# A conditioning product moved from TensorE to VectorE in a three-block transformer kernel

## The reference, cut to what matters

```python
def ada_params(cond, w_ada, b_ada):
    m = jax.nn.silu(cond) @ w_ada + b_ada
    return jnp.split(m[..., None, :], 6, axis=-1)      # shift, scale, gate, twice
...
def modulate(x, g, shift, scale):
    return rmsnorm_2(x, g) * (1 + scale) + shift
...
    x = x + g_m * y
    x = x + g_f * ec_moe(modulate(x, norm_ffn[l], sh_f, sc_f), ...)
```

## Time and profile before

| | |
|---|---|
| three runs | 2081.14, 2081.37, 2082.59 us (median 2081.37) |
| the profiled execution | 2083.17 us, its span on the core 2081.4 us |
| TensorE busy | 1675.8 us (81%) |
| weight loads of TensorE | 788.9 us (38%) |
| VectorE busy | 424.6 us (20%) |
| ScalarE busy | 310.4 us (15%) |
| GpSimd busy | 74.4 us (4%) |
| dense stages | 0 to 249, 720 to 993, 1458 to 1606 us |
| moved from main memory | 709.09 MB |

### The profile page before, as it was taken

How to read it: one execution, slowest core, us unless ns; L and a number is a source line. 1 busy time by engine, 2 the same in 40 slices (tenths; PEclk the granted TensorE clock), 3 DMA queues, 4 the chain that set the end, 5 groups by cost and what they waited for, 6 DMA issues and landing times.

```text
span 2081.4 us, 22500 instructions
## 1 busy us (share of the span) xinstructions
PE 1675.8 (81%) x9286; PEld 788.9 (38%) x9286; DVE 424.6 (20%) x941; ACT 310.4 (15%) x723; POOL 74.4 (4%) x113
## 2 busy tenths in 40 slices
PE   7999988888888689999786776776997776767766
PEld 3456544433343244664331321321784231313212
DVE  2234311111111142154210111111213111111101
ACT  2123111111111121251110100100101110100000
POOL 1300000000000042000000000000000000000000
PEclk9978999999999989999988988988998998988988
DMA  9464699999999942464999999999742999999997
GB/s 348 162 242 162 242 413 422 421 421 422 423 422 421 405 173 74 157 247 176 384 420 420 420 425 420 420 422 414 279 162 81 380 424 421 421 420 425 420 420 324
DMA packets 129436, 711.46 MB, mean 342 GB/s; under 512 B 5568, under 2 KB 5824, under 8 KB 104640
## 3 DMA queue, kind: packets, MB, share of 16 engines
q1 hardware_dynamic: 128496, 707.02, 83.9%
q10 hardware_dynamic: 848, 3.15, 0.4%
HBM read 709.09 MB, written 1.05 MB: 341 GB/s over the span
## 4 chain that ended last, share of the span: by engine, by line
DMA 46%; PE 45%; DVE 2%; ACT 2%; issue 2%; POOL 1%; ACTq 0%; POOLq 0%; SPq 0%; DVEq 0%
DMA ring<-in_moe_w_down 33%; DMA ring<-in_w_down 8%; PE bank L446 8%; PE bank L1252 6%; DMA ring<-in_moe_w_up 5%; PE bank L1207 5%; PE bank L1894 4%; PE bank L566 4%; PE bank L1123 4%; PE bank L1276 4%; PE bank L362 2%; PE bank L382 1%; PE bank L694 1%; PE bank L308 1%; PE bank L1648 1%
## 5 line engine op out<-in xcount | busy, mean ns | idle before, releaser
L1207 PE MATMUL bank<-ring,arena 128*32 128x512 f32 x3072 | 401.1, 650 | 150.8 <-DMA ring<-in_moe_w_up 108.3
L1252 PE MATMUL bank<-ring,arena 128*32 128x512 f32 x1536 | 225.7, 714 | 157.8 <-DMA ring<-in_moe_w_down 117.1
L1276 PE MATMUL bank<-arena 128*128 128x512 f32 x512 | 235.3, 602 | 30.9 <-DVE arena L1331 17.4
L1207 PEld LDWEIGHTS bank<-ring,arena 128*32 128x32 f32 x3072 | 93.4, 113 | 384.3 <-issue 242.7
L1298 DVE COPY arena<-bank 128x512 f32<-128x512 f32 x96 | 66.4, 692 | 672.1 <-PE bank L1207 672.1
L1252 PEld LDWEIGHTS bank<-ring,arena 128*32 128x32 f32 x1536 | 49.3, 120 | 291.3 <-issue 177.7
L446 PE MATMUL bank<-ring,hT 128*128 128x512 f32 (+1 forms) x352 | 153.0, 591 | 3.1 <-DVE hT L323 1.6
L1290 ACT ACTIVATE arena<-bank 128x512 f32<-128x512 f32 x96 | 57.3, 597 | 624.8 <-PE bank L1207 624.8
L1276 PEld LDWEIGHTS bank<-arena 128*128 128x128 f32 x512 | 92.3, 190 | 138.2 <-issue 94.0
L1123 PEld LDWEIGHTS bank<-arena,xn 128*128 128x128 f32 x512 | 124.1, 333 | 7.1 <-issue 3.3
L1123 PE MATMUL bank<-arena,xn 128*128 128x128 f32 x512 | 123.0, 400 | 1.0 <-DVE arena L1155 0.7
(11 more groups left out here) (226 smaller groups left out, 1207.4 us busy)
## 6 DMA issues: line engine op xcount, KB each, us to landing
ring<-in_moe_w_gate SPq DMA_DIRECT2D x64, 2048.0 KB, 24.2
ring<-in_moe_w_up SPq DMA_DIRECT2D x64, 2048.0 KB, 26.3
ring<-in_moe_w_down SPq DMA_DIRECT2D x64, 2048.0 KB, 26.9
ring<-in_w_gate SPq DMA_DIRECT2D x32, 2048.0 KB, 19.2
ring<-in_w_up SPq DMA_DIRECT2D x32, 2048.0 KB, 21.6
ring<-in_w_down SPq DMA_DIRECT2D x32, 2048.0 KB, 24.3
ring<-in_ada_w SPq DMA_DIRECT2D x24, 2048.0 KB, 10.2
ring<-in_w_in SPq DMA_DIRECT2D x6, 2048.0 KB, 20.3
```

The lines of the kernel that those rows point to most:

```text
L1207: last = nc.tensor.matmul(AA[hf if M.nf == 2 else up][32 * j:32 * j + 32, :], xgT[:, x + kk, a:a + C], w[:, kq + j, hf * NC:(hf + 1) * NC] ...
L1252: last = nc.tensor.matmul(AA[n][32 * j:32 * j + 32, :], act_s[:, b, q * C:(q + 1) * C], w[:, j, n * NC:(n + 1) * NC], start=(kk < 4), stop ...
L1276: nc.tensor.matmul(Y[2 * t + n][:, :], wselT[:, e % 2, t * P:(t + 1) * P], z_s[:, n * NC:(n + 1) * NC], start=(e == 0 and M.fresh), stop=( ...
```

## The change

The product is computed on VectorE. For each section and vector, eight instructions add weight rows times a number per partition into an accumulator of 128 x 1024 (`ada_add_dve`): the first a `tensor_scalar`, the others `scalar_tensor_tensor` with the weights and the accumulator in on-chip memory. There are 14 such jobs (sections 0 and 1 twice), 112 instructions. What stays on TensorE is the sum over the 128 partitions: two matmuls of 512 columns with ones for a gate, eight transposes for a shift or scale, which VectorE then reduces with two instructions. ScalarE's copies go. An accumulator lies in a buffer of its own or in one that is free then.

A weight item is now half of a section, all 1024 columns of 512 rows, so that a descriptor moves 4 KB where it moved 2 KB. The slot is released by VectorE's last add that reads it. The items are spread between the projection chunks of all three dense stages: sections 0 to 2 in block one, 3 to 7 in block two, 8 to 11 in block three (which had none). The adds are written into the step lists: in a query or key unit one before the unit and one inside `rooted`, between VectorE's sum and its wait for GpSimd's root; two to four in the value units; some in the attention loops. The loads of the gate biases for block three and of the context rows are issued later, since their buffers serve as accumulators.

```diff
-EARLY = 4
+JOBS = [(s, c) for s in range(12) for c in range(2 if s < 2 else 1)]
+ADDS = [(s, c, k) for s in range(12) for half in range(2) for c in range(2 if s < 2 else 1) for k in range(4 * half, 4 * half + 4)]
...
+    after = [[(0, 0)], [(0, 1)], [], [(1, 0)], [(1, 1)], [(2, 0), (2, 1)]]
+    for n, name in enumerate(CHUNKS1):
+        proj("proj1", n, ("w_in", W_IN_COLS[name]))
+        for sec, half in after[n]:
+            conditioning(sec, half)
...
+    after = [[(3, 0)], [(3, 1), (4, 0)], [(4, 1), (5, 0)], [(5, 1), (6, 0)], [(6, 1), (7, 0), (7, 1)]]
...
+    after = [[(8, 0), (8, 1)], [(9, 0)], [(9, 1), (10, 0)], [(10, 1), (11, 0), (11, 1)], [], []]
...
-        def rooted(ins, sums, n):
+        def rooted(ins, sums, n, meanwhile=None):
 
             dve_step(ins)
             sums_added(sums, n)
+            if meanwhile is not None:
+                meanwhile()
             nc.vector.wait_ge(roots_done, chain_at["sums"])
...
+        def ada_add_dve(count):
+
+            dve = nc.vector
+            for _ in range(count):
+                sec, c, k = ADDS[chain_at["adds"]]
+                chain_at["adds"] += 1
+                i = ITEM["ada", sec, k // 4]
+                j = job_at[sec, c]
+                acc, w, by = accs[acc_of[j]], ring[i % SLOTS][:, :, :].rearrange("p a b -> p (a b)")[:, (k % 4) * D:(k % 4 + 1) * D], condT[:, k, c:c + 1]
+                if k % 4 == 0:
+                    wait_item(dve, i)
+                if k:
+                    dve.wait_ge(ada_added, add_at[sec, c, k - 1])
+                    ins = dve.scalar_tensor_tensor(acc, w, by, acc, ALU.mult, ALU.add)
+                else:
...
+                    ins = dve.tensor_scalar(acc, w, by, None, ALU.mult)
+                ins.then_inc(ada_added, 1)
...
+        def ada_sum_pe(j, banks):
...
+            if sec % 6 in (G_M, G_F):
                 for n in range(2):
+                    last = nc.tensor.matmul(banks[n][:, :], const("ones"), acc[:, n * NC:(n + 1) * NC], start=True, stop=True)
             else:
                 for k in range(KD):
+                    last = nc.tensor.transpose(banks[k // 4][:, (k % 4) * P:(k % 4 + 1) * P], acc[:, k::KD], ident)
...
+            for n in range(2):
+                ins = dve.tensor_reduce(dst[:, 4 * n:4 * n + 4], banks[n][:, :].rearrange("p (k r) -> p k r", r=P), AX.X, ALU.add)
...
         def steps1():
             for u in range(len(units1)):
+                if u:
+                    yield "ada_add", 1 if u < 9 else 4
                 yield "proj", u
                 if u >= 2:
                     yield "tr", u - 2
+                if u in (8, 10):
+                    yield "ada_sum", (8, 10).index(u)
+                if u in (9, 11):
+                    yield "ada_use", (9, 11).index(u)
+            yield "ada_add", 4
...
+                if u in (3, 8, 24):
+                    yield "ada_sum", 2 + (3, 8, 24).index(u)
+                if u in (6, 11, 27):
+                    yield "ada_use", 2 + (6, 11, 27).index(u)
+                if u % 2 and u < 16:
+                    yield "ada_add", 1
...
         def steps2():
             for u in range(NU2):
+                yield "ada_add", 1 if units2[u]["kind"] == "qk" else 2
                 yield "proj", u
...
+                if u in (6, 10, 14):
+                    yield "ada_sum", 5 + (6, 10, 14).index(u)
...
+                if u in (1, 7):
+                    yield "ada_sum", 8 + (1, 7).index(u)
+                if u in (2, 8):
+                    yield "ada_use", 8 + (2, 8).index(u)
+                if u < 4:
+                    yield "ada_add", 1
...
                 last.then_inc(item_done, 1)
+                if i >= 2:
+                    ada_sum_pe(8 + i, TR)
             out_pe(2, 0, mix3, [(mix_done, 8)])
...
+            ada_add_dve(12)
             for n in range(2):
...
+                if n == 0:
+                    ada_use_dve(10, TR)
+                    ada_add_dve(6)
+                    ada_use_dve(11, TR)
+                    ada_add_dve(8)
...
+                    if what[0] == "ada":
+                        w = ada_w[what[1]][:, what[2] * D:(what[2] + 1) * D].rearrange("(p k) n -> p k n", p=P)
```

More of the change, by code:

```diff
@@ new lines, in transformer_blocks @@
+        add_at = {a: n + 1 for n, a in enumerate(ADDS)}
+        job_at = {j: n for n, j in enumerate(JOBS)}
+        accs = {"own": ada_acc[:, :], "ctx0": gate_rows[:, 1, 0, :], "ctx1": gate_rows[:, 1, 1, :], "end": arena[:, ARENA - D:ARENA],
+                "odd": arena[:, 9472:9472 + D]}
+        acc_of = ["own", "ctx0", "ctx1", "end", "own", "own", "ctx1", "own", "ctx1", "own", "odd", "own", "odd", "own"]
+        for sec in range(12):
+            for half in range(2):
+                released[ITEM["ada", sec, half]] = (ada_added, add_at[sec, 1 if sec < 2 else 0, 4 * half + 3])
@@ L395, in ada_use_dve @@
+                dve.tensor_tensor(g[:, NC:D], g[:, NC:D], banks[1][:, :], ALU.add).then_inc(ada_used, 1)
                 return
-            sums = AB[0][:, 0:2 * KD].rearrange("p (k c) -> p c k", c=2)
             m = (0 if sec < 3 else 2) + sec % 3
-            both = [(mod[:, l, m, :], 0)] + ([(mod_ctx[:, m, :], 1)] if s < 2 else [])
-            for n, (dst, c) in enumerate(both):
-                ins = nc.vector.tensor_tensor(dst, sums[:, c, :], col(f"b{l}{sec}"), ALU.add)
-                if sec % 3 == 1:
-                    dve_step(ins)
-                    gain = col(f"norm_mix{l}" if sec < 3 else f"norm_ffn{l}")
-                    ins = nc.vector.scalar_tensor_tensor(dst, dst, 1.0, gain, ALU.add, ALU.mult)
+            dst = mod_ctx[:, m, :] if c else mod[:, l, m, :]
@@ L405, in ada_use_dve @@
+            for n in range(2):
+                ins = dve.tensor_reduce(dst[:, 4 * n:4 * n + 4], banks[n][:, :].rearrange("p (k r) -> p k r", r=P), AX.X, ALU.add)
+            dve_step(ins)
+            ins = dve.tensor_tensor(dst, dst, col(f"b{l}{sec}"), ALU.add)
+            if sec % 3 == 1:
+                dve_step(ins)
+                gain = col(f"norm_mix{l}" if sec < 3 else f"norm_ffn{l}")
+                ins = dve.scalar_tensor_tensor(dst, dst, 1.0, gain, ALU.add, ALU.mult)
             ins.then_inc(ada_used, 1)
@@ L476, in post_dve @@
                 dve.wait_ge(sqs, q + 1)
[L477 removed]
+                rooted(nc.vector.tensor_reduce(s8, view(sq[:, q % 2, 0:n]), AX.X, ALU.add), s8, HD, meanwhile)
                 if q >= 2:
@@ L1046, in route2_dve @@
                 dve_step(v.match_replace(workT, best8, workT, -1.0))
-                if n == 1 and section is not None:
-                    ada_use_dve(section)
             dve_step(v.memset(onesT, 1.0))
@@ L1068, in route2_pe @@
             last.then_inc(af_tr, 1)
-            if section is not None:
-                ada_sum_pe(section)
-                ada_mm_pe(section + 1)
             pe.wait_ge(af_slot, l + 1)
```

243 lines of the change are left out of this document (102 added, 141 removed).

## The result

The changed kernel takes **2089.83 us** (median of 7 runs, 2088.32 to 2093.18), the kernel before in the same comparison 2081.25 (7 runs): ratio 1.0041, 95% interval 1.003 to 1.0053, so it is slower by 6 to 11 us. The forecast was 2080.5 (no change) in a range of 2059 to 2095. The range holds the time; that the kernel would become slower was missed. The profiled execution took 2088.69 with a span of 2086.6, 5.2 more than the span before; it lies 1.1 under its median, the one before lay 1.8 above the median of its first three runs, which is why the medians stand further apart (8.6 us) than the profiles. What follows accounts for the 5.2.

A forecast was written before the change was run, and what follows sets the result against it. Expert stages were taken as bound by weight loads, so only dense stages, mostly TensorE-bound, counted: -22.5 + 14 + 3.5 + 3.7 = -1.3 us. From the 2081.37 median that gave 2080.1, stated as 2080.5, range 2059 to 2095.

The forecast's parts named there:

- Block 1, attention loop: First attention loop: products, ScalarE copies and small sums go, so 81.5 us becomes 59, a gain of 22.5 us.
- nine microseconds at half clock: First attention loop, second half: 3.5 heads go at half clock, the other 12.5 at full, together 26.5 us.
- half clock to the end of that loop: Rival, first attention loop: without the conditioning products the clock stays at half, loop 73.5 us, kernel time 2095 us; chance 0.20.
- bound for full clock throughout: First attention loop: lower bound of 54 us if TensorE kept full clock all through, against 59 forecast.
- Block 1, projections: Block 1 before its attention loop: adds hold GpSimd and delay the last chunk's load, a loss of 14 us.
- powers of 2.9 us: Sign in the profile after: GpSimd's powers in the units take near 2.9 us instead of 1.64.
- Block 2: Whole second dense stage: projections +9.8 and +3.5, attention loop -7.5, routing -2.3, together +3.5 us.
- Block 3: Third dense stage: four sums join a TensorE that is never idle, a loss of 3.7 us.
- Routing of block 1: Block 1's routing: removed products and sums save about 3 us, half clock costs 3, so nothing; bounds -3 and +2.
- the adds do not hold GpSimd: Rival: VectorE's adds leave GpSimd free; block 1 regains 11.4 us, block 2 about 9, kernel time 2060 us; chance 0.17.
- full clock: Rival: full clock through the first attention loop, 54 us instead of 59, kernel time 2075.5 us; chance 0.18.
- fuller rings: Rival: earlier expert loads let expert stages start ahead, 5 us per stage at most, kernel time 2071 us; chance 0.05.

The follow-up runs named there:

- e4: Changed kernel with block 2's first four units free of adds, their eight adds moved to later units and sums moved back; ratio 1.0019 against the kernel before.
- e1: Changed kernel plus four bursts of four 512-column matmuls, results thrown away, before heads 7, 13, 18, 29 of the first attention loop; ratio 1.0042 against the kernel before.
- e7: Changed kernel plus three bursts of four 512-column matmuls at heads 10, 18 and 26 of the first attention loop; ratio 0.9999 against the kernel before.
- e10: Changed kernel with loads reordered, adds and sums re-placed (none beside heads 18 to 31), bursts of four matmuls at head 18, two at 26; 2071.5 us, ratio 0.9949.
- e3: Changed kernel with only block 1's load order altered, so the last projection chunk no longer waits for the 16th add; ratio 1.0012 against the kernel before.
- e11: Changed kernel with block 2's first eight adds summing in two PSUM banks, one section's product left out; 2083.19 us, one execution only.
- e6: Changed kernel with block 1's loads reordered, adds moved away from busy rope units, and three bursts of four matmuls at heads 10, 18, 26; ratio 0.9966.
- e8: Changed kernel with loads reordered, adds and sums re-placed (14 adds in the first loop), bursts of four matmuls at head 16, two at 27; ratio 0.9981.
- e12: Kernel before the change plus one burst of four 512-column matmuls at head 16 of its first attention loop; ratio 1.0015 against the kernel before.
- e2: Changed kernel with every add turned into a product alone with one SBUF input, conditioning sums left out; ratio 0.9965 against the kernel before.

## Why the prediction was right or wrong

**Block 1, attention loop, -22.5: wrong, this is the step that failed.** I rebuilt the loop with "nine microseconds at half clock" in its second half and the other 12.5 heads at full. That number was taken from the stretch at 188 to 197 in the old loop, where the clock rose with no L362 block, and one such rise was made the rule. The changed loop was at 0.50 from 125 to 178, through head 23, and rose behind a burst that I had priced at 1.7 us, its time at full clock, and not seen as one: the two matmuls of the gate sum, which took 3.73. Seven us later it was at half again. The waits were not the error: the sum allowed 6 us for them and TensorE stood 5.1. Measured 72.5 us; my bound for half clock throughout was 73.5, and e4, where that happened, took 74.7. The rival "half clock to the end of that loop" is nearly what happened, with its mechanism and its loop time; it had a chance of 0.20 against 0.40. It deserved the larger one: three of the four rises in the old loop came inside an L362 block, and the change removed all of L362. It also removed the L382 sums, inside which the clock fell three times in the old loop; in the new one it was low all the same. e1, e7 and e10 show the cause by giving bursts back. The bound for full clock throughout, 54, does not follow from the sum's own rows: heads at 0.8 and 1.4 and sums at full rate give some 45. No run held full clock through the whole loop, so neither is tested.

**Block 1, projections, +14: right in kind, too large.** Measured +8.4. The adds hold GpSimd, 1.15 and 1.0 us of their 1.28 each, since each begins some 0.15 us ahead of the instruction that it holds. The 6.86 us of the earlier trace rows are the second block's; in the first the chain without the adds is 6.5 us long, with a pause of 0.3 to 0.9 behind it that the adds use up. So the unit is 8.7 us and not 9.4 (78.77 less the unit before's 70.07). The 16th add ended at 92.5 and not 97, and the load took 9.2 us for my 10.2: TensorE restarts 6.6 us late, not 11.5 (11.9 by the prediction's own 107 and 95.14). The half-rate unit cost 2.6 us (9.61 for 7.03), not 1.6, the sum 0.9 as said, and the forget bias gave back nearly 2 us that I had not seen (L683 in 3.69 us at full clock; L667 took 5.5, most of it at half). e3 shows the mechanism. The sign that I named, powers of 2.9 us, was wrong: the adds meet the rope. Powers of 2.1 to 2.6 us stand ahead of the rope units, in the queries and keys without a rope, and the chain that ends in the last chunk's load runs through them (L258 at 40.83, 2.61 us); they are part of the 2 us of lag that the sum gave these units.

**Block 2: right.** 2.1 us a unit in the GpSimd chain where I took two times 1.28; with the sums +11.8 for +13.3. Attention -8.3 for -7.5, routing -2.1 for -2.3.

**Block 3: right**, +3.1 for +3.7. **Routing of block 1: right**, +0.3 for 0.

**Together:** a loop 13.5 us too optimistic, projections 5.6 us and block 2 and 3 2.7 us too pessimistic, and the expert stages 1.0 longer by chance: with 0.3 of routing that is -1.3 + 13.5 - 5.6 - 2.7 + 1.0 + 0.3 = 5.2, the difference of the two spans. The rival "the adds do not hold GpSimd" (2060) is refuted by the rope's times in the changed kernel and by e11, where they are free again; "full clock" (2075.5) by the window of the loop; "fuller rings" by the expert stages, none of which is shorter by more than 0.8 us.

## What to carry to other kernels

Before dense matmuls are taken out of a loop of small ones, look at where TensorE's clock rises in the trace: if it rises behind just those, expect the rest of the loop at half rate, and work out the gain with half-rate rows. Work moved to VectorE has to be placed by GpSimd's timeline as well as VectorE's, one unit behind included; a sum kept in PSUM leaves GpSimd alone. Dummy bursts paid here only where few were used, most of them over waits of TensorE, and little made it stand behind them (e6, e7, e10); elsewhere they cost what they gave or more (e1, e8, e12).

## What was not expected of the hardware

A TensorE that is busy 45.00 of 48.00 us with dependent products of 64 and 128 columns stays at 0.50 of its clock for all of it; in e4 it stays there for the whole loop, though from 151.5 to 200.7 it is busy without any gap (49.20 of 49.20 us). The bursts of four matmuls that began at half all raised it; the gate sum of two raised it in the changed kernel and not in e4. It then held for 25 us of the larger heads (e10), where the waits add up to 0.9 us. It fell within 1.1 us of the end of waits of 1.33 (e8) and 1.59 us (the changed kernel), but in e1 also at 148.7, among the smaller heads, with a wait of 0.30 ahead of it. What exactly it asks for is not settled by these runs. The holding between VectorE and GpSimd goes both ways: an 8-column instruction of 0.17 us took 1.19 beside GpSimd's sum. And a VectorE product with one input, at double rate, holds GpSimd for 0.6 us (e2), where two inputs were thought to be needed.
